# Two heads' attention scores, and the clearing of a buffer, move from one stage into the stage before it

## The reference, cut to what matters

```
mk, mv = memory_kv(mem_prompt, mem_norm[i], w_xkv[i], xk_norm[i])        # 256 memory rows
xp = xp + cross_attn(rmsnorm(xp, norm_cross[i]), mk, mv, ...)            # prompt: own memory
xs = xs + cross_attn(rmsnorm(xs, norm_cross[i]), cache_mem_k[i], cache_mem_v[i], ...)   # samples: cached memory

def cross_attn(h, mk, mv, w_xq, xq_norm, w_xo):
    q = rmsnorm((h @ w_xq).reshape(b, t, X_HEADS, X_HEAD), xq_norm)
    a = softmax(einsum('bthd,bmhd->bhtm', q, mk) * X_HEAD ** -0.5)
    return einsum('bhtm,bmhd->bthd', a, mv).reshape(b, t, D_MODEL) @ w_xo
```

## Time and profile before

| | us |
|---|---|
| median of 3 runs | 2209.18 (2209.09 to 2216.57) |
| the profiled execution's own time | 2210.32 |
| its span, first to last instruction | 2208.4 |
| mean granted TensorE clock | 0.941 of 2.4 GHz |
| `attention`, layer 0 | begins at 622.1, next stage at 681.1 |
| `attention`, layer 1 | begins at 1717.8, next stage at 1777.4 |

### The profile page before, as it was taken

How to read it: one execution, slowest core, us unless ns; L and a number is a source line. 1 busy time by engine, 2 the same in 40 slices (tenths; PEclk the granted TensorE clock), 3 DMA queues, 4 the chain that set the end, 5 groups by cost and what they waited for, 6 DMA issues and landing times. The chain is left out here.

```text
span 2208.4 us, 40404 instructions
## 1 busy us (share of the span) xinstructions
PE 2013.3 (91%) x17801; PEld 1875.7 (85%) x17801; DVE 1222.5 (55%) x1509; ACT 498.6 (23%) x840; POOL 230.9 (10%) x221
## 2 busy tenths in 40 slices
PE   7998659979989999999999989776799799999999
PEld 6997449879957999999999955465799589999999
DVE  5884564558445655554467445455674455555532
ACT  2221434242132111110021044432322321111000
POOL 3110122012001000000110011021220010000000
PEclk9998758989999999999999989777899999999999
DMA  5221100024472222232222340200343722222321
GB/s 186 87 77 62 38 20 4 1 70 144 153 305 68 87 94 86 95 107 92 77 89 86 95 156 0 86 2 15 110 157 126 304 79 94 86 95 95 102 92 65
DMA packets 52400, 209.10 MB, mean 95 GB/s; under 512 B 6450, under 2 KB 7090, under 8 KB 46258
## 3 DMA queue, kind: packets, MB, share of 16 engines
q1 hardware_dynamic: 52274, 207.30, 27.6%
HBM read 193.88 MB, written 13.40 MB: 94 GB/s over the span
## 5 line engine op out<-in xcount | busy, mean ns | idle before, releaser
L483 PE MATMUL ps<-mx_hi,w_hi 128*128 128x260 f32 x2560 | 520.7, 285 | 18.1 <-DVE w_lo L460 9.6
L483 PE MATMUL ps<-mx_hi,w_lo 128*128 128x260 f32 x2560 | 516.5, 283 | 0.0
L483 PE MATMUL ps<-mx_lo,w_hi 128*128 128x260 f32 x2560 | 516.0, 283 | 0.0
L483 PEld LDWEIGHTS ps<-mx_hi,w_hi 128*128 128x128 f32 x2560 | 396.1, 189 | 22.3 <-DVE w_lo L460 9.8
L483 PEld LDWEIGHTS ps<-mx_hi,w_lo 128*128 128x128 f32 x2560 | 395.8, 189 | 0.0
L483 PEld LDWEIGHTS ps<-mx_lo,w_hi 128*128 128x128 f32 x2560 | 394.9, 189 | 0.0
L458 DVE CAST w_hi<-w 128x1024 fp32r<-128x1024 f32 (+1 forms) x256 | 188.4, 736 | 300.9 <-PE ps L483 300.7
L460 DVE TENSOR_TENSOR w_lo<-w,w_hi 128x1024 fp32r<-128x1024 f32 (+1 forms) x256 | 330.6, 1291 | 8.8
L483 PE MATMUL ps<-hid_hi,w_hi 128*128 128x260 f32 x704 | 141.8, 283 | 0.0
L483 PE MATMUL ps<-hid_hi,w_lo 128*128 128x260 f32 x704 | 141.7, 283 | 0.0
L483 PE MATMUL ps<-hid_lo,w_hi 128*128 128x260 f32 x704 | 141.3, 282 | 0.0
(11 more groups left out here) (491 smaller groups left out, 2830.4 us busy)
## 6 DMA issues: line engine op xcount, KB each, us to landing
w<-in_w_gu SPq DMA_DIRECT2D x88, 512.0 KB, 3.6
w<-in_w_in SPq DMA_DIRECT2D x56, 512.0 KB, 3.6
w<-in_w_down SPq DMA_DIRECT2D x32, 704.0 KB, 4.1
w<-in_w_xkv SPq DMA_DIRECT2D x32, 512.0 KB, 3.8
scr<-in_mem_k SPq DMA_DIRECT2D x10, 1024.0 KB, 6.9
scr<-in_mem_v SPq DMA_DIRECT2D x10, 1024.0 KB, 14.8
w<-in_w_out SPq DMA_DIRECT2D x16, 512.0 KB, 3.7
w<-in_w_xq SPq DMA_DIRECT2D x16, 512.0 KB, 4.0
```

Of the source, the lines that this page charges most:

```text
L483: ins = nc.tensor.matmul(self.ps[:, 2 * (o % 2) + s, 0:b - a], w[:, k, :], v[:, x, a:b], start=first, stop=last)
```

## The change

PE's scores of heads 0 and 1 leave `attention` and are issued at the end of `out_memory_query`: three quarters of head 0 between the sums of heads 2 and 3, the rest after the sums of head 3. POOL clears the query blocks at the end of its list there. In `attention` PE begins with the wait for DVE's copy and the sample scores; DVE begins with the copy, without a wait for POOL. Everything else keeps its order.

```diff
+    SCORE_BANK = (0, 6)
+    def prompt_scores(self, pe, h, chunks):
+        q = self.c[:, self.X_Q:self.X_Q + KT]
+        kv = self.flat(self.X_KV)[:, 0:16 * MEM].rearrange("p (a m) -> p a m", a=16)
+        for t in chunks:
+            for j in range(2):
+                ins = self.nc.tensor.matmul(self.ps[:, self.SCORE_BANK[h % 2] + t // 2, (t % 2) * MEM:(t % 2 + 1) * MEM],
+                                            q[:, 2 * h + j, t * P:(t + 1) * P], kv[:, 2 * h + j], start=j == 0, stop=j == 1)
+        return ins
...
@@ out_memory_query
+            self.scores_at = self.take(self.scores_ready, 4)
...
                 head_sums(2)
+                pe.wait_ge(self.keys_scaled.sem, self.keys_scaled.at(1))
+                pe.wait_ge(self.head_scaled.sem, self.head_scaled.at(1))
+                self.tile_read(pe, legs[2], KT - 2)
+                self.prompt_scores(pe, 0, range(NC - 1))
                 head_sums(3)
+                self.prompt_scores(pe, 0, range(NC - 1, NC)).then_inc(self.scores_ready.sem, 1)
+                pe.wait_ge(self.head_scaled.sem, self.head_scaled.at(2))
+                pe.wait_ge(self.head_scale.sem, self.head_scale.at(3))
+                self.prompt_scores(pe, 1, range(NC)).then_inc(self.scores_ready.sem, 1)
...
+                self.pool.step(nc.gpsimd.memset(self.query_blocks(), 0.0))
...
@@ attention
             def _(pool):
-                self.pool.tell(nc.gpsimd.memset(one_query, 0.0), self.pool_out)
...
-                scores(0)
-                scores(1)
                 pe.wait_ge(self.sample_vector.sem, self.sample_vector.at(1))
...
-                dve.wait_ge(self.pool_out.sem, self.pool_out.at(1))
                 self.dve.tell(nc.vector.tensor_copy(diagonal(one_query), q[:, :, T:N]), self.sample_vector)
                 maxima(0)
```

More of the change, by code:

```diff
@@ L667, in memory_rows, with query_blocks @@
         return self.flat(self.X_A)[:, 0:KT * MEM].rearrange("p (k m) -> p k m", k=KT)
+    SCORE_BANK = (0, 6)
[7 more added lines that the diff above has]
+        return ins
+    def query_blocks(self):
+        return self.o[:].rearrange("p a b -> p (a b)")[:, 0:KT * B * 32]
     def out_memory_query(self, i):
@@ L2172, in attention @@
         scale = 1.0 / 16
-        one_query = self.o[:].rearrange("p a b -> p (a b)")[:, 0:KT * B * 32]
+        one_query = self.query_blocks()
         one_weight = self.flat(self.X_KV)[:, 0:KT * B * 32]
@@ L2189, in attention @@
         HP = 4
-        score_bank = (0, 6)
+        score_bank = self.SCORE_BANK
         with self.stage() as block:
@@ L2206, in _ @@
             def _(pool):
-                self.pool.tell(nc.gpsimd.memset(one_query, 0.0), self.pool_out)
                 pool.wait_ge(self.stored.sem, self.stored.count)
-                pool.wait_ge(self.scores_ready.sem, self.scores_ready.at(HP))
+                pool.wait_ge(self.scores_ready.sem, self.scores_at + HP)
                 self.pool.tell(nc.gpsimd.memset(one_weight, 0.0), self.pool_out)
@@ L2214, in scores @@
                 def scores(h):
[L2215 to L2222, removed]
+                    pe.wait_ge(self.exp_ready.sem, self.exp_ready.at(h - 1))
+                    self.prompt_scores(pe, h, range(NC)).then_inc(self.scores_ready.sem, 1)
                 def sample_scores(b0):
@@ L2293, in _ @@
                 row_transposes(1)
-                self.scores_ready.count += HP
                 self.keys_used.count += B
@@ L2335, in _ @@
                 transposed(1)
-                act.wait_ge(self.pool_out.sem, self.pool_out.at(2))
+                act.wait_ge(self.pool_out.sem, self.pool_out.at(1))
                 act.wait_ge(self.sample_tensor.sem, self.sample_tensor.at(1))
@@ L2359, in maxima @@
                     p = h % 2
-                    dve.wait_ge(self.scores_ready.sem, self.scores_ready.at(h + 1))
+                    dve.wait_ge(self.scores_ready.sem, self.scores_at + h + 1)
                     self.dve.step(nc.vector.tensor_reduce(
```

## The result

The changed kernel takes 2217.03 us, median of 20 runs, beside 2214.01 for 20 runs of the kernel before (the three shown above are among them): ratio 1.0019, 95% interval 1.0011 to 1.0028. By the ratio that is 4.2 us slower (0.0019 x 2214), between 2.4 and 6.2; the two medians are 3.0 apart. Its profiled execution took 2216.82, span 2214.9. Taking 9.4 us of PE work per layer off the head of the attention made the kernel a little slower.

What follows compares the result with a forecast made beforehand. PE, busy 91% of the span, was taken to bound the kernel. Per layer -9.42 removed, +1.7 stage, +7.7 transfer waits, +2.0 clock make +2.0, +4.0 in all: 2213 us, range 2206 to 2219.

Steps and rivals of the forecast that it cites:

- The transfers hold: Attention, before head 2's scores: the net gain of 7.7 us is all spent in key waits of 3.4 and 2.9; gain 0.
- The clock: Head 2's scores after the key waits: PE's clock drops, costing 2.0 us per layer, bounds 0 and 2.32.
- 4.6: The clock cost by the Trainium skill's rule for matmul groups parted by transfer waits: twice 2.32, +4.6 us.
- The row at 638 to 640: Profile row before the change: clock 1.00 through a wait of 0.79 us; by it alone the clock would cost 0.
- The keys of sample 7: Attention, layer 0: these keys still land at 639.7, so head 2's scores start where they start today.
- land behind the store (633.23) in any case: Keys of sample 6, layer 0: issued 1.7 us later, yet landing at 635.87 behind the store of the prompt's keys.
- The stage's end: Query stage, layer 0: ends about 1.7 us later with the added scores; the next stage begins at 623.8, not 622.1.
- The clearing: POOL at the end of the query stage: 1.80 us, covered by PE's new end at 623.5, so it costs nothing.
- The value loads: SP, behind the keys of sample 7: six value loads queued in a row; cost 0, bounds 0 and 2.64 us.
- rival 3: Value loads take bandwidth from sample 7's keys: 2218.5 with one transfer ahead (chance 0.13), 2223.8 with two (0.04).
- rival 4: Query stage: moved scores run slow or hold up head 3, stage ends at up to 629.6; no chance of its own.
- The sum: Whole kernel: +2.0 us per layer, +4.0 in all, giving a median of 2213, 0.2% slower.

Runs made afterwards that it cites:

- experiment 3: The changed kernel with the stores of the prompt's values and keys issued in the query stage as soon as ready: 2197.03 us, ratio 0.9935 to the kernel before.
- experiment 5: The changed kernel with 24 of the 32 records of the moved scores left out: 2216.67 us, ratio 1.0007 to the kernel before.
- experiment 1: The changed kernel with 11 and 5 extra matmuls in the waits for the keys of samples 6 and 7: 2214.05 us, ratio 1.0012 to the kernel before.
- experiment 4: The changed kernel with scores of heads 2 and 3 and transposes of head 1 ahead of samples 6 and 7: 2202.64 us, ratio 0.9957 to before.
- experiment 7: The changed kernel with the key load of sample 6 issued right behind the store of the prompt's keys, in the query stage: 2216.43 us, one run.
- experiment 6: The kernel before with only the clearing of the query blocks moved to the stage before: 2212.41 us, ratio 1.0000 to the kernel before.

## Why the prediction was right

*The transfers hold.* Forecast: all of the 7.7 us ends in waits for the keys of samples 6 and 7. They are 5.63 and 1.72 long, not 3.4 and 2.9: head 0's softmax is done sooner (5.37 from maxima to result instead of 6.36, transposes at 628.84, not 630.5), and the scores of sample 6 run at the lower clock and take a microsecond of the second wait. The sum of the waits is as forecast within 1.1, and nothing is gained. Experiments 3 and 5 show the cause from both sides.

*The clock.* Forecast 2.0 per layer; measured 1.6 (0.87 on the sample scores, 0.72 to 0.74 on head 2), as experiment 1 shows by taking it away. The forecast laid all of it on the scores of head 2; more than half falls on those of sample 7 ahead of them, which it had at full clock. So the clock went as the Trainium skill has it (TensorE: Matmul & The Clock Gate, "HAM oscillation — how this bites in real kernels"): 0.50 in 634 to 636, between groups of matmuls parted by waits for transfers. Its price over both layers is 3.2, not 4.6. The row at 638 to 640, with its short wait, was the wrong guide for waits of this length.

*The keys of sample 7.* Forecast: they stay at 639.7 because nothing ahead of them moves. Counted from the first key load they come 0.89 later in layer 0 and 0.23 earlier in layer 1, 0.3 on average; in layer 1 their own transfer takes 6.0, before 7.3. The step "land behind the store (633.23) in any case" is off by a little: the store lands 17.0 to 17.9 after its issue in the changed kernel and in experiments 1, 4, 5 and 7, and 15.9 to 16.1 in the kernel before and experiment 6. The transfers were not slower for it: from the first key load to the store's landing they moved 364 GB/s over 19.9 us in layer 0, before 357 over 18.7. But in the five kernels where the store lands late 7.2 to 7.3 MB had been moved by then, in the other two 6.7. So about half a megabyte more had gone ahead of the store's end, and all that SP had issued behind it is the keys of sample 6. Why is open.

*Costs put at nothing.* The stage's end: the next one begins at 623.53 on the old scale (623.12 + 0.41), forecast 623.8. The clearing: nothing, by experiment 6. The value loads: the prediction read only the first of them and took them to come one by one, but in the kernel before six were already issued behind the keys of sample 7 within 5.2 us, now within 4.0. The keys land in 6.1 and 6.0, before in 6.4 and 7.3, so rival 3 did not come; what a burst beside single loads would cost, no run shows. The 629.6 of rival 4 is too high: it sets 9.42, the time of 32 records that ran only in part at the lower clock, for the 16 of head 1. Nothing in the sum uses it.

*The sum.* 1.6 + 0.3 is 1.9 per layer, 3.8 in all; forecast 4.0, measured 4.2. That it fits so well is in part luck: the clock cost 0.4 less per layer than forecast, the late keys 0.3 more. The 2213 itself stood on the median of three runs, 2209.18; with 20 runs that median is 2214.01, so the 4 us are to be compared and not the 2213. The two profiled executions differ by 6.5, more than that: in the changed one the first outputs ran at the lower clock in both layers (5.33 for 3.70), in the other in neither, 3.3 us. This I had not forecast. In the kernels with the outputs in their old place it happened in 13 of 18 stages, among them 3 of 6 of the kernels whose scores were not moved, so it belongs to no one version. In those with moved scores it was 10 of 12; whether the change makes it more frequent, and so has a part in the 4.2, is open.

## What to carry to other kernels

A small wait for a transfer late in a stage (0.79 and 1.41 us here) says that little can be won by what is taken out ahead of it: look for what issues that transfer, and what it queues behind, before shortening the work. Work that covered the time of a transfer was not free to remove, because the engine then idled long enough to lose its clock (1.6 us per layer). The order of payment matters: with the stores out of the way the same edit was worth 13 us.

## What the runs showed of the hardware

The same small wait sometimes costs the clock and sometimes not: ahead of the first outputs PE idles 2.1 to 2.5, works 0.4 to 0.7 and idles 0.48 in all these kernels, and in 13 of 18 stages the following matmuls took 5 to 6 us, in the others 3.70. A store of 1 MB queued behind 5 MB of other transfers lands 15.9 to 17.9 us after its issue, 4.9 when it is issued ahead of them, and SP's wait for it held back the load that SP had next. Useless matmuls in two waits for transfers kept the clock at 1.00 from 630 to 644, where it had fallen to 0.50 without them.
